# A decoder trunk with a product-key expert layer: one-hot tables compared in batches, the early expert rows summed through diagonal matrices

## The chip, the core and the metric

The kernel runs on one NeuronCore of a Trainium2 chip. The core has five engines that run side by side, each through its own list of instructions in order, and that meet only at semaphores: TensorE (PE: matrix products; PEld is its loading of weights), VectorE (DVE), ScalarE (ACT), GpSimd (POOL) and SyncE (SP, which here issues transfers). Sixteen DMA engines move data between the device memory and the on-chip memory SBUF; PSUM banks take the products of PE. The metric is the device time of one execution in microseconds (us), lower is better, as the median of several runs.

## What is computed

Two layers over 512 tokens of width 1024, in float32. Each layer runs four mixers (state space, linear recurrence, RWKV-7, sparse attention) and then the expert layer (PEER). Only the expert layer is touched:

```python
def peer_ffn(x, wq, keys, u, v):
    ...
    q = (xt @ wq).reshape(t, PEER_HEADS, 2, PEER_KEY_DIM)
    sc = jnp.einsum('thcd,hcnd->thcn', q, keys).astype(jnp.float32)
    s1, i1 = lax.top_k(sc[:, :, 0], PEER_TOPK)
    s2, i2 = lax.top_k(sc[:, :, 1], PEER_TOPK)
    cand = (s1[..., :, None] + s2[..., None, :]).reshape(t, PEER_HEADS, PEER_TOPK * PEER_TOPK)
    cidx = (i1[..., :, None] * PEER_NKEYS + i2[..., None, :]).reshape(t, PEER_HEADS, PEER_TOPK * PEER_TOPK)
    top, pos = lax.top_k(cand, PEER_TOPK)
    eidx = jnp.take_along_axis(cidx, pos, axis=-1)
    gate = jax.nn.softmax(top, axis=-1)
    ...
        act = jax.nn.gelu(jnp.einsum('td,tkd->tk', xb, u[ib]))
        return jnp.einsum('tk,tkd->td', gb * act, v[ib])
```

Each of the 512 tokens picks 128 of 16384 experts (8 heads, 16 each: the best 16 of the 256 sums of 16 and 16 key scores). An expert is a row of `u` and a row of `v`, 1024 floats each; the token's output is the sum over its picks of gate times gelu(x·u) times v.

## The kernel before

The expert layer of one layer is the function `experts`, run once per layer. Its four chunks of 128 tokens are treated in two ways at once.

**Sparse chunks 0 and 1.** There are 256 *steps*, one for each chunk and pick. In a step POOL gathers, for each of the 128 tokens of the chunk, the row of its expert (u and v together, 8 KB) with one indirect DMA of 1 MB (`gather`, L1795) into one of 7 slots; DVE forms the product with x and its sum (`dot`, L1958), ACT takes the gelu of two steps at a time (L1889), and 4 steps later (LAG) DVE multiplies the gate in (L1966) and adds coefficient times v row to the sum `h` (`add_row`, L1970). The gather of step n+3 waits until the sum of step n-4 has freed its slot.

**Dense chunks 2 and 3.** All experts are computed in 128 *tiles* of 128 experts: PE multiplies the tile's u with the 256 tokens (`with_u`, L1848), ACT takes the gelu (L1895), DVE multiplies with the tile's gates (L1978), PE multiplies with the tile's v into banks 4 to 7 (`with_v`, L1859). A u tile and a v tile of 512 KB each are loaded for each. The gates, mostly zeros, are made beforehand in 64 *quads* of 4 tokens: for each token two one-hot tables of 128x128, `hot1` (comparison of an iota with the first key index, times the gate) and `hot2` (comparison with the second key index), and PE multiplies one with the other (`spread_quad`, L1837). ACT copies the result out (L1915), every fourth quad 1 MB goes to device memory (`gates`), and the dense tiles read it back by expert. Of a quad's `hot1`, DVE makes two tables (L1950) and POOL two (L1805), each in one instruction with comparison and gate; `hot2` is made by ACT as relu(1 - (i - n)²), four squares (L1903) and one relu (L1907).

**Order.** All engines walk through the same 212 *beats*, an order written out by numbers: `choose_chunk` (top 16 of the sums and their expert indices, on DVE) of chunk 0 ahead of the beats, of chunk 2 from beat 0, of chunk 3 from beat 14, of chunk 1 from beat 84, in 14 pieces, a piece in each beat; quads in beats 16 to 79; tiles' v products from beat 84; `steps_until(beat)` and `u_until(beat)` say how many steps and u tiles are done by a beat: a step in two of three beats of the quads, 20 u tiles ahead of the dense part, one in every three beats up to beat 60. Within a beat each engine's list has its own order. On POOL: its half of `hot1` of the quad, then the gather. On PE: the quad, then a u tile, then a v tile. On DVE: the piece of the choice, its half of `hot1`, dot, sum, gate of a tile. Within two quads the tables and banks alternate: `hot1` of quad q waits for the product of quad q-2 (`spread`), and the product of q waits for the copy of q-2.

Of the kernel before, what the change touches and what calls it, by code (L numbers as in the profile page):

```python
# [21 lines left out]
P = 128  # L22
# [1473 lines left out]
PICKS = HEADS * TOP  # L1496
ORDER = (0, 2, 3, 1)
# [7 lines left out]
ACTS = 22  # L1505
OWN_ACTS = 14
RUN_AHEAD = 20
# [20 lines left out]
def steps_until(beat):  # L1528

    chosen = CHOOSE_AT[3] + PIECES  # L1530
    if beat <= TILES_AT - 4:
        return max(beat, 0) // 3 + max(beat - chosen, 0) // 3
    first = (TILES_AT - 4) // 3 + (TILES_AT - 4 - chosen) // 3 + 4
    if beat <= TILES_AT:
        return first + beat - TILES_AT
# [120 lines left out]
def choose_chunk(nc, k, p, s, dve, mark, settle, t):  # L1656
# [6 lines left out]
    mark(nc.vector.tensor_tensor(p.sums[:, :, :, :], best[:, :, 0, :].unsqueeze(3).to_broadcast([P, HEADS, TOP, TOP]),  # L1663
                                 best[:, :, 1, :].unsqueeze(2).to_broadcast([P, HEADS, TOP, TOP]), ALU.add))
    settle()
    yield
    rest = p.rest[:, :, :].rearrange("p n w -> p (n w)").rearrange("p (n w) -> p n w", n=2)
    for first in range(0, HEADS, 2):
        heads = range(first, first + 2)
        values = {h: p.sums[:, h, :, :].rearrange("p a b -> p (a b)") for h in heads}  # L1670
        for h in heads:
            mark(nc.vector.max(out=p.top[:, h, 0:8], in_=values[h]))
        settle()
        for h in heads:
            nc.vector.max_index(out=p.where[:, h, 0:8], in_max=p.top[:, h, 0:8], in_values=values[h])
            mark(nc.vector.match_replace(out=rest[:, h % 2, :], in_to_replace=p.top[:, h, 0:8], in_values=values[h], imm_value=-3.0e38))
        settle()
        for h in heads:
            mark(nc.vector.max(out=p.top[:, h, 8:16], in_=rest[:, h % 2, :]))
        settle()  # L1680
        for h in heads:
            mark(nc.vector.max_index(out=p.where[:, h, 8:16], in_max=p.top[:, h, 8:16], in_values=rest[:, h % 2, :]))
        settle()
        yield
# [4 lines left out]
    mark(nc.vector.tensor_scalar(p.rank[:, 0, :], flat, 4, None, ALU.logical_shift_right))  # L1689
# [37 lines left out]
def experts(nc, k, p, A, l):  # L1727
# [3 lines left out]
    with stage(nc, "dve_done", "shifted", "exps", "indexed", "chosen", "turned", "kept", "hot1", "hot1_pool", "squared", "hot2", "spread", "copied",  # L1731
               "stored0", "stored1", "u_done", "gelus_u", "gated", "v_done", "dots", "gelus", "coefs", "summed", "y_added",
# [55 lines left out]
        def _(pool):  # L1788
# [31 lines left out]
        def _(pe):  # L1820
# [8 lines left out]
            def spread_quad(q):  # L1829
                pe.wait_ge(s["hot1"], q + 1)  # L1830
# [31 lines left out]
            for beat in range(BEATS):  # L1862
# [11 lines left out]
        def _(act):  # L1874
# [47 lines left out]
            for beat in range(BEATS):  # L1922
# [10 lines left out]
                if 0 <= beat - QUADS_AT < QUADS:  # L1933
                    second_hots(beat - QUADS_AT)
# [6 lines left out]
        def _(dve):  # L1941
            mark, settle = counted(dve, s["dve_done"])

            def first_hots(q):
# [4 lines left out]
                for n in range(2):  # L1949
# [204 lines left out]
```

## Time and profile before

| | us |
|---|---|
| median of 3 runs | 4028.96 (4024.53 to 4030.17) |
| the profiled execution, its own time | 4015.8 |
| its span, first to last instruction | 4014.1 |
| first layer: choice starts | 778.4 |
| first layer: first and last quad's product start | 867.9, 1102.6 |
| first layer: dense part, first to last v product | 1126.8 to 1986.4 |
| second layer: last quad's product starts | 3099.1 |
| second layer: last v product starts | 3982.0 |

The busy shares of the page (PE 79%, DVE 63%, POOL 27%) are means over stages of different kinds. The expert layers cover some 1210 us of each layer of about 1990, in two clear stages: the quads, in which POOL is the busiest engine, and the dense part, in which the DMA engines are. The page's list of the chain that ended last covers 0% of the span here and says nothing; the stages are read from windows and from the order of instructions in time.

### The profile page before, as it was taken

What the parts mean: (1) busy time and instruction counts of PE and PEld (TensorE: products, weight loads), DVE (VectorE), ACT (ScalarE), POOL (GpSimd) and SP (SyncE); (2) the same over time, 40 slices, a digit from 0 to 9 for tenths busy, and PEclk for the clock granted to TensorE, in tenths of its full rate; (3) what the DMA queues carried; (4) which work ended last, traced back from release to release, by engine and by line L of the source; (5) the groups of instructions that cost most, each with busy time, mean ns of one, the idle gap of its engine ahead of it and who ended that gap; (6) DMA issues with size and microseconds to landing.
All of it is one profiled execution on the core that took longest, in us unless ns stands there. A gap on an engine that the chain in (4) does not pass through costs nothing. (4 is left out here: it accounts for less than half of the span.)

```text
span 4014.1 us, 39261 instructions
## 1 busy us (share of the span) xinstructions
PE 3166.3 (79%) x12836; PEld 2265.1 (56%) x12836; DVE 2544.6 (63%) x5150; ACT 933.6 (23%) x2020; POOL 1102.9 (27%) x1016
## 2 busy tenths in 40 slices
PE   6947677737689999999678477776476899999995
PEld 5725566636556665666266255665365566656662
DVE  3674544896686666666646645348966866666666
ACT  2331133137800000000033311231487000000000
POOL 0012111238922222222200121122498222222221
PEclk9969688868689999999889796888686999999997
DMA  3100112149899999999821001121498999999997
GB/s 103 49 0 1 46 34 82 58 143 317 288 356 411 417 416 417 417 416 406 320 94 37 0 1 46 43 79 58 173 320 284 366 415 417 417 417 417 413 403 303
DMA packets 235342, 943.29 MB, mean 235 GB/s; under 512 B 19584, under 2 KB 85632, under 8 KB 164864
## 3 DMA queue, kind: packets, MB, share of 16 engines
q0 software_dynamic: 73728, 536.90, 33.6%
q1 hardware_dynamic: 95360, 370.31, 24.1%
q10 hardware_dynamic: 66048, 33.56, 2.9%
q8 instruction: 102, 1.67, 0.2%
q14 instruction: 104, 0.85, 0.1%
HBM read 904.52 MB, written 35.65 MB: 234 GB/s over the span
## 5 line engine op out<-in xcount | busy, mean ns | idle before, releaser
L1848 PE MATMUL bank<-peer_x_late,xT 128*128 128x256 f32 x4096 | 987.3, 397 | 146.7 <-ACT peer_acts_u L1895 86.2
L1848 PEld LDWEIGHTS bank<-peer_x_late,xT 128*128 128x128 f32 x4096 | 818.3, 201 | 368.9 <-issue 174.6
L1795 POOL DMA_INDIRECT peer_slots<-in_peer_uv,peer_rows x512 | 542.3, 1059 | 1551.8 <-DVE h L1970 1412.7
L1958 DVE CUSTOM_DVE_ANT_0 peer_slots<-peer_slots,wide 128x1024 f32<-128x1024 f32 x512 | 627.4, 1225 | 512.7 <-DMA peer_slots<-in_peer_uv,peer_rows 511.7
L1970 DVE SCALAR_TENSOR_TENSOR h<-peer_slots,peer_coef,h 128x1024 f32<-128x1024 f32 x512 | 656.9, 1283 | 9.3
L1859 PE MATMUL bank<-ring,peer_acts_u 128*128 128x512 f32 x1344 | 616.9, 605 | 48.6 <-issue 33.3
L1859 PEld LDWEIGHTS bank<-ring,peer_acts_u 128*128 128x128 f32 x1344 | 259.8, 194 | 323.6 <-issue 301.6
L1805 POOL TENSOR_SCALAR peer_hot<-iota,peer_picks 128x128 f32<-128x128 f32 x256 | 329.6, 1294 | 23.7 <-PE bank L1837 20.7
L1837 PE MATMUL bank<-peer_hot 128*128 128x128 f32 x1024 | 195.7, 356 | 176.3 <-ACT peer_hot L1907 65.4
L1889 ACT ACTIVATE peer_coef<-peer_dots 128x2 f32<-128x2 f32 x256 | 51.2, 201 | 1201.1 <-DVE peer_dots L1958 1197.5
L1859 PE MATMUL bank<-ring,wide 128*128 128x512 f32 x704 | 321.1, 601 | 11.3 <-DVE wide L1978 9.9
L1837 PEld LDWEIGHTS bank<-peer_hot 128*128 128x128 f32 x1024 | 175.3, 257 | 195.8 <-issue 138.0
L1859 PEld LDWEIGHTS bank<-ring,wide 128*128 128x128 f32 x704 | 134.6, 192 | 153.5 <-issue 146.3
L1950 DVE TENSOR_SCALAR peer_hot<-iota,peer_picks 128x128 f32<-128x128 f32 x256 | 85.5, 384 | 142.7 <-PE bank L1837 142.0
L190 PE MATMUL bank<-mix_x_hi,w_hi 128*128 128x512 f32 x384 | 154.3, 402 | 12.6 <-DVE w_lo L280 12.6
L1903 ACT ACTIVATE peer_hot<-iota,peer_picks 128x128 f32<-128x128 f32 x512 | 161.9, 390 | 7.4 <-ACT peer_staging L1915 7.3
L1603 POOL TENSOR_TENSOR peer_w_lo<-ring,peer_w_hi 128x1024 fp32r<-128x1024 f32 x32 | 76.4, 2391 | 315.1 <-ACT peer_w_hi L1588 315.1
L191 PE MATMUL bank<-mix_x_lo,w_hi 128*128 128x512 f32 x384 | 153.0, 398 | 0.0
L192 PE MATMUL bank<-mix_x_hi,w_lo 128*128 128x512 f32 x384 | 152.9, 398 | 0.0
L1895 ACT ACTIVATE peer_acts_u<-bank 128x256 f32<-128x256 f32 x168 | 61.8, 378 | 365.9 <-PE bank L1848 363.4
L1915 ACT COPY peer_staging<-bank 128x512 f32<-128x512 f32 x128 | 131.5, 1027 | 57.4 <-PE bank L1837 51.1
L280 DVE TENSOR_TENSOR w_lo<-ring,w_hi 128x1024 fp32r<-128x1024 f32 x48 | 58.6, 1225 | 115.2 <-ACT w_hi L260 115.1
(449 smaller groups left out, 4190.0 us busy)
## 6 DMA issues: line engine op xcount, KB each, us to landing
xT<-in_peer_ut SPq DMA_DIRECT2D x256, 512.0 KB, 18.2
ring<-in_peer_uv SPq DMA_DIRECT2D x256, 512.0 KB, 18.3
gates<-peer_staging ACTq DMA_DIRECT2D x32, 1024.0 KB, 7.1
peer_staging<-gates SPq DMA_DIRECT2D x32, 1024.0 KB, 20.8
ring<-in_w_in SPq DMA_DIRECT2D x48, 512.0 KB, 3.5
ring<-in_peer_wq SPq DMA_DIRECT2D x32, 512.0 KB, 3.5
nsa_w<-in_cmp_w SPq DMA_DIRECT2D x2, 4096.0 KB, 12.1
ring<-in_w_out SPq DMA_DIRECT2D x16, 512.0 KB, 4.2
```

The costliest lines, as they stand in the source:

```text
L190: nc.tensor.matmul(out, left[0], right[0], start=first, stop=False)
L191: nc.tensor.matmul(out, left[0], right[1], start=False, stop=False)
L192: return nc.tensor.matmul(out, left[1], right[0], start=False, stop=last)
L1795: nc.gpsimd.indirect_dma_start(out=p.slots[:, n % ROW_SLOTS, :], out_offset=None, in_=A["peer_uv"], in_offset=bass.IndirectOffsetOnAxis(ap ...
L1805: last = nc.gpsimd.tensor_scalar(p.hot1[:, 4 * (q % 2) + n, :], k.iota128[:, :], p.picks[:, 0, 4 * q + n:4 * q + n + 1], p.picks[:, 2, 4 * ...
L1837: last = nc.tensor.matmul(k.bank[2 + q % 2][:, n * P:(n + 1) * P], p.hot2[:, at, :], p.hot1[:, at, :], start=True, stop=True)
L1848: last = nc.tensor.matmul(k.bank[bank_of[j]][:, 0:DENSE], u_raw[:, j % U_RING, b * P:(b + 1) * P], p.x_late[:, b, :], start=b == 0, stop=b ...
L1859: last = nc.tensor.matmul(k.bank[4 + 2 * t + half][:, :], act_of(j)[:, t * P:(t + 1) * P], k.ring[:, j % V_RING, half * 512:(half + 1) * 5 ...
L1903: last = nc.scalar.activation(hot[:, n, :], k.iota128[:, :], ACT.Square, scale=-1.0, bias=p.picks[:, 1, 4 * q + n:4 * q + n + 1])
L1915: nc.scalar.copy(spread[:, g % 2, :, at:at + 4].rearrange("p j t -> p t j"), k.bank[2 + q % 2][:, :].rearrange("p (t j) -> p t j", t=4)).t ...
L1958: nc.vector.tensor_tensor_reduce(out=u, in0=u, in1=k.wide[:, t, :], scale=1.0, scalar=0.0, op0=ALU.mult, op1=ALU.add, accum_out=p.dots[:, ...
L1970: nc.vector.scalar_tensor_tensor(out=k.h[:, t, :], in0=p.slots[:, m % ROW_SLOTS, DM:2 * DM], scalar=p.coef[:, t, pick:pick + 1], in1=k.h[: ...
```

## The change

There is no change to what goes in and out. `hot1` and `hot2` of a quad are each made by DVE in one comparison of 128x512 (`hots`), without the gate. The gate is then multiplied into the four tables of `hot1` one by one: three by ACT (`gates`, an activation with Copy and a scale), one by POOL (`last_gate`). ACT's squares and relus fall away. PE's product waits for both (`hot1_act`, `hot1_pool`).

For the first 48 steps (EARLY) the sum is no longer DVE's: POOL multiplies the identity with the coefficients of the step (`diagonal`), and PE multiplies this diagonal with the v rows of the slot, adding up in banks 5 and 6 (`add_row` on PE). PE then counts the step as summed. Before the dense tiles DVE adds the two banks to `h` once (`take_early`).

The choice takes the best 16 of 112 sums (the 4 best first keys with all 16 second ones, and the other 12 with the 4 best second ones) rather than of 256, in groups of four heads, with some more small instructions that turn the position into ranks; it has 12 pieces. The numbers of the order: chunk 3 from beat 12, quads in beats 14 to 77, dense tiles from beat 82; a step in three of four beats from beat 24 on (52 steps before the dense part, where there were 47); u tiles one per beat from the start, up to 18, and 20 rather than 22 buffers for activations.

```diff
+PAIRS = 4 * TOP + 12 * 4
...
-ACTS = 22
-OWN_ACTS = 14
-RUN_AHEAD = 20
+ACTS = 20
+OWN_ACTS = 12
+RUN_AHEAD = 18
...
-CHOOSE_AT = {2: 0, 3: 14, 1: 84}
-PIECES = 14
-EXPS_AT = {2: 6, 3: 20, 1: 90}
-TURN_AT = {2: 15, 3: 30}
-KEEP_AT = {2: 16, 3: 31}
-QUADS_AT = 16
-TILES_AT = 84
+CHOOSE_AT = {2: 0, 3: 12, 1: 82}
+PIECES = 12
+EXPS_AT = {2: 4, 3: 16, 1: 86}
+TURN_AT = {2: 12, 3: 24}
+KEEP_AT = {2: 13, 3: 25}
+QUADS_AT = 14
+TILES_AT = QUADS_AT + QUADS + 4
...
+    if beat <= chosen:
+        return beat // 3
+    first = chosen // 3
     if beat <= TILES_AT - 4:
-        return max(beat, 0) // 3 + max(beat - chosen, 0) // 3
-    first = (TILES_AT - 4) // 3 + (TILES_AT - 4 - chosen) // 3 + 4
+        return first + (beat - chosen) * 3 // 4
...
+EARLY = steps_until(TILES_AT) - LAG
+DIAGONALS = 4
...
-        return max(0, min(RUN_AHEAD, (beat + 1) // 3))
+        return max(0, min(RUN_AHEAD, beat))
...
+    sums = p.sums[:, :, :, :].rearrange("p h a b -> p (h a b)")[:, 0:HEADS * PAIRS].rearrange("p (h n) -> p h n", h=HEADS)
+    for at, rows, cols in ((0, slice(0, 4), TOP), (4 * TOP, slice(4, TOP), 4)):
+        n = rows.stop - rows.start
+        mark(nc.vector.tensor_tensor(sums[:, :, at:at + n * cols].rearrange("p h (a b) -> p h a b", b=cols),
+                                     best[:, :, 0, rows].unsqueeze(3).to_broadcast([P, HEADS, n, cols]),
+                                     best[:, :, 1, 0:cols].unsqueeze(2).to_broadcast([P, HEADS, n, cols]), ALU.add))
...
+    for first in range(0, HEADS, 4):
+        heads = range(first, first + 4)
...
+    mark(nc.vector.tensor_scalar(p.rank[:, 0, :], flat, 6, None, ALU.logical_shift_right))
...
-            def first_hots(q):
+            def last_gate(q):
                 if q % (QUADS // 2) == 0:
                     pool.wait_ge(s["kept"], q // (QUADS // 2) + 1)
-                if q >= 2:
-                    pool.wait_ge(s["spread"], q - 1)
-                for n in range(2, 4):
-                    last = nc.gpsimd.tensor_scalar(p.hot1[:, 4 * (q % 2) + n, :], k.iota128[:, :], p.picks[:, 0, 4 * q + n:4 * q + n + 1],
-                                                   p.picks[:, 2, 4 * q + n:4 * q + n + 1], ALU.is_equal, ALU.mult)
-                last.then_inc(s["hot1_pool"], 1)
+                pool.wait_ge(s["hot1"], q + 1)
+                hot = p.hot1[:, 4 * (q % 2) + 3, :]
+                nc.gpsimd.tensor_scalar(hot, hot, p.picks[:, 2, 4 * q + 3:4 * q + 4], None, ALU.mult).then_inc(s["hot1_pool"], 1)
+            def diagonal(m):
+                t, pick = m // PICKS, m % PICKS
+                pool.wait_ge(s["coefs"], m // BATCH + 1)
+                if m >= DIAGONALS:
+                    pool.wait_ge(s["summed"], m - DIAGONALS + 1)
+                nc.gpsimd.tensor_scalar(p.diagonal[:, m % DIAGONALS, :], k.ident[:, :], p.coef[:, t, pick:pick + 1], None,
+                                        ALU.mult).then_inc(s["diagonals"], 1)
...
-                    first_hots(beat - QUADS_AT)
+                    last_gate(beat - QUADS_AT)
                 for n in now(steps_until, beat):
+                    if LAG <= n < LAG + EARLY:
+                        diagonal(n - LAG)
                     if n >= LAG and n - LAG + ROW_SLOTS < STEPS:
                         gather(n - LAG + ROW_SLOTS)
...
-                pe.wait_ge(s["hot1"], q + 1)
+                pe.wait_ge(s["hot1_act"], q + 1)
...
+            def add_row(m):
+                pe.wait_ge(s["diagonals"], m + 1)
+                for half in range(2):
+                    last = nc.tensor.matmul(k.bank[5 + half][:, :], p.diagonal[:, m % DIAGONALS, :],
+                                            p.slots[:, m % ROW_SLOTS, DM + half * 512:DM + (half + 1) * 512],
+                                            start=m == 0, stop=m == EARLY - 1)
+                last.then_inc(s["summed"], 1)
...
+                    pe.wait_ge(s["early_in"], 2)
...
+                for n in now(steps_until, beat):
+                    if LAG <= n < LAG + EARLY:
+                        add_row(n - LAG)
...
-            def second_hots(q):
-
-                hot = p.hot2[:, 4 * (q % 2):4 * (q % 2) + 4, :]
-                if q >= 2:
-                    act.wait_ge(s["spread"], q - 1)
-                for n in range(4):
-                    last = nc.scalar.activation(hot[:, n, :], k.iota128[:, :], ACT.Square, scale=-1.0,
-                                                bias=p.picks[:, 1, 4 * q + n:4 * q + n + 1])
-                last.then_inc(s["squared"], 1)
-                act.wait_ge(s["squared"], q + 1)
-                nc.scalar.activation(hot, hot, ACT.Relu, scale=-1.0, bias=k.ones[:, 0:1]).then_inc(s["hot2"], 1)
+            def gates(q):
+
+                act.wait_ge(s["hot1"], q + 1)
+                for n in range(3):
+                    hot = p.hot1[:, 4 * (q % 2) + n, :]
+                    last = nc.scalar.activation(hot, hot, ACT.Copy, scale=p.picks[:, 2, 4 * q + n:4 * q + n + 1])
+                last.then_inc(s["hot1_act"], 1)
...
-            def first_hots(q):
+            def hots(q):
                 if q % (QUADS // 2) == 0:
                     dve.wait_ge(s["kept"], q // (QUADS // 2) + 1)
                 if q >= 2:
                     dve.wait_ge(s["spread"], q - 1)
-                for n in range(2):
-                    last = nc.vector.tensor_scalar(p.hot1[:, 4 * (q % 2) + n, :], k.iota128[:, :], p.picks[:, 0, 4 * q + n:4 * q + n + 1],
-                                                   p.picks[:, 2, 4 * q + n:4 * q + n + 1], ALU.is_equal, ALU.mult)
-                last.then_inc(s["hot1"], 1)
+                for n, (hot, made) in enumerate(((p.hot1, "hot1"), (p.hot2, "hot2"))):
+                    at = 4 * (q % 2)
+                    nc.vector.tensor_tensor(hot[:, at:at + 4, :], k.iota128[:, :].unsqueeze(1).to_broadcast([P, 4, P]),
+                                            p.picks[:, n, 4 * q:4 * q + 4].unsqueeze(2).to_broadcast([P, 4, P]),
+                                            ALU.is_equal).then_inc(s[made], 1)
...
-                if m:
-                    dve.wait_ge(s["summed"], m)
+                if m < EARLY:
+                    return
...
+            def take_early():
+                dve.wait_ge(s["summed"], EARLY)
+                for half in range(2):
+                    o = slice(half * 512, (half + 1) * 512)
+                    nc.vector.tensor_tensor(k.h[:, 0, o], k.h[:, 0, o], k.bank[5 + half][:, :], ALU.add).then_inc(s["early_in"], 1)
+                dve.wait_ge(s["early_in"], 2)
```

POOL in the middle of the quads, five beats before and four beats after. In `peer_hot` both tables of one-hots are named (here it is `hot1`). Before:

```order
L1805 TENSOR_SCALAR peer_hot<-iota,peer_picks 128x128 x4
L1795 DMA peer_slots<-in_peer_uv,peer_rows 128x2048
L1805 TENSOR_SCALAR peer_hot<-iota,peer_picks 128x128 x2
L1795 DMA peer_slots<-in_peer_uv,peer_rows 128x2048
L1805 TENSOR_SCALAR peer_hot<-iota,peer_picks 128x128 x4
```

After:

```order
L1830 TENSOR_SCALAR peer_hot<-peer_hot,peer_picks 128x128 x2
L1836 TENSOR_SCALAR peer_diagonal<-ident,peer_coef 128x128
L1821 DMA peer_slots<-in_peer_uv,peer_rows 128x2048
L1830 TENSOR_SCALAR peer_hot<-peer_hot,peer_picks 128x128
L1836 TENSOR_SCALAR peer_diagonal<-ident,peer_coef 128x128
L1821 DMA peer_slots<-in_peer_uv,peer_rows 128x2048
L1830 TENSOR_SCALAR peer_hot<-peer_hot,peer_picks 128x128
```

One table a quad stands where two stood, and a diagonal stands directly in front of each gather.

PE at the end of its early u tiles, at the start of the quads (`peer_x_late,xT` is a u tile, eight instructions each; `peer_chosen` the turning of the choice). Before:

```order
L1848 MATMUL bank<-peer_x_late,xT 128x256 x40
L1826 MATMUL bank<-ident,peer_chosen 128x128 x3
L1837 MATMUL bank<-peer_hot 128x128 x4
L1848 MATMUL bank<-peer_x_late,xT 128x256 x8
L1837 MATMUL bank<-peer_hot 128x128 x12
```

After:

```order
L1880 MATMUL bank<-peer_x_late,xT 128x256 x96
L1858 MATMUL bank<-ident,peer_chosen 128x128 x3
L1880 MATMUL bank<-peer_x_late,xT 128x256 x16
L1869 MATMUL bank<-peer_hot 128x128 x4
L1887 MATMUL bank<-peer_slots,peer_diagonal 128x512 x2
L1880 MATMUL bank<-peer_x_late,xT 128x256 x8
L1869 MATMUL bank<-peer_hot 128x128 x4
```

Twelve u tiles stand ahead of the first turning rather than five, 14 ahead of the first quad, and a step's sum follows its beat's quad.

## Rows read from the trace of the kernel before

**Rows 1.** Windows of 50 us, first layer: busy us of each engine, clock, DMA.

```profile
core 0: us, PE busy (x) PEld busy (x) DVE busy (x) ACT busy (x) POOL busy (x), PEclk, DMA share, GB/s
800.00:850.00 50.00, 15.17 (x48) 12.05 (x48) 48.67 (x93) 3.74 (x6) 8.22 (x7) 0.62 0.44 168
...
1050.00:1100.00 50.00, 27.95 (x110) 24.53 (x111) 31.29 (x61) 40.15 (x88) 47.96 (x37) 0.50 0.80 265
...
1300.00:1350.00 50.00, 50.00 (x178) 33.48 (x177) 33.89 (x51) 3.13 (x13) 12.18 (x13) 1.00 1.02 417
```

**Rows 2.** PE through the quads in time: start, us, what, idle before and releaser.

```profile
907.11 2.04 PE L1837 MATMUL bank<-peer_hot 128*128 128x128 f32 x8 [2.64 <-ACT peer_hot L1907]
...
912.94 1.95 PE L1837 MATMUL bank<-peer_hot 128*128 128x128 f32 x16
...
928.26 1.13 PE L1837 MATMUL bank<-peer_hot 128*128 128x128 f32 x8 [2.76 <-ACT peer_hot L1907]
929.23 3.62 PE L1848 MATMUL bank<-peer_x_late,xT 128*128 128x256 f32 x16
```

**Rows 3.** The last quads and the four beats behind them, PE, POOL and DVE in time.

```profile
1095.81 2.75 POOL L1805 TENSOR_SCALAR peer_hot<-iota,peer_picks 128x128 f32<-128x128 f32 x2
...
1098.66 2.05 PE L1837 MATMUL bank<-peer_hot 128*128 128x128 f32 x8 [2.38 <-issue]
...
1102.60 2.04 PE L1837 MATMUL bank<-peer_hot 128*128 128x128 f32 x8 [1.89 <-issue]
...
1106.04 1.28 DVE L1970 SCALAR_TENSOR_TENSOR h<-peer_slots,peer_coef,h 128x1024 f32<-128x1024 f32 x1
...
1107.59 0.94 POOL L1795 DMA_INDIRECT peer_slots<-in_peer_uv,peer_rows  x1 [2.23 <-DVE h L1970]
```

**Rows 4.** POOL in time: the first tables, and the steady order in the quads.

```profile
860.12 3.14 POOL L1805 TENSOR_SCALAR peer_hot<-iota,peer_picks 128x128 f32<-128x128 f32 x4
...
929.66 1.02 POOL L1795 DMA_INDIRECT peer_slots<-in_peer_uv,peer_rows  x1 [0.16 <-issue]
930.73 2.51 POOL L1805 TENSOR_SCALAR peer_hot<-iota,peer_picks 128x128 f32<-128x128 f32 x2
```

**Rows 5.** PE in the dense part: the v products of two tiles.

```profile
1150.07 3.60 PE L1859 MATMUL bank<-ring,peer_acts_u 128*128 128x512 f32 x8
```

**Rows 6.** Groups of instructions of the whole run, with mean ns of one.

```profile
L1805 POOL TENSOR_SCALAR peer_hot<-iota,peer_picks 128x128 f32<-128x128 f32 x256 | 329.6, 1294 | 23.7 <-PE bank L1837 20.7
...
L1903 ACT ACTIVATE peer_hot<-iota,peer_picks 128x128 f32<-128x128 f32 x512 | 161.9, 390 | 7.4 <-ACT peer_staging L1915 7.3
...
L1978 DVE TENSOR_TENSOR peer_acts_u<-peer_acts_u,peer_staging 128x256 f32<-128x256 f32 x168 | 70.1, 419 | 20.4 <-DMA peer_staging<-gates 20.4
...
L1699 DVE TENSOR_TENSOR peer_sums<-peer_rank_f,iota 128x2048 f32<-128x2048 f32 x16 | 36.7, 2291 | 0.1
```

**Rows 7.** DVE: ranking of 128 columns, then the choice of chunk 0, in time.

```profile
774.83 0.87 DVE L1648 MAX8 peer_best<-peer_rest 128x8 f32<-128x128 f32 x4
...
778.36 2.29 DVE L1663 TENSOR_TENSOR peer_sums<-peer_best 128x2048 f32<-128x2048 f32 x1 [1.48 <-PEq L71]
780.69 0.75 DVE L1672 MAX8 peer_top<-peer_sums 128x8 f32<-128x256 f32 x2
...
784.89 0.75 DVE L1672 MAX8 peer_top<-peer_sums 128x8 f32<-128x256 f32 x2
...
812.59 0.29 DVE L1711 TENSOR_SCALAR peer_chosen<-peer_chosen,first_row 128x128 f32<-128x128 f32 x1
...
814.24 2.29 DVE L1663 TENSOR_TENSOR peer_sums<-peer_best 128x2048 f32<-128x2048 f32 x1
```

**Rows 8.** PE before the quads: two u tiles, the turning, the first quad.

```profile
840.59 9.41 PE L1848 MATMUL bank<-peer_x_late,xT 128*128 128x256 f32 x32 [34.83 <-ACT peer_acts_u L1895]
853.95 0.55 PE L1826 MATMUL bank<-ident,peer_chosen 128*128 128x128 f32 x3 [3.95 <-DVE peer_chosen L1722]
867.86 2.08 PE L1837 MATMUL bank<-peer_hot 128*128 128x128 f32 x8 [13.37 <-DVE peer_hot L1950]
```

More of the change, by code:

```diff
@@ L1515 @@
 READ = 8
[L1518 to L1524 removed]
+CHOOSE_AT = {2: 0, 3: 12, 1: 82}
[5 more added lines that the diff above has]
+TILES_AT = QUADS_AT + QUADS + 4
 BEATS = TILES_AT + TILES
 def steps_until(beat):
+    beat = max(beat, 0)
     chosen = CHOOSE_AT[3] + PIECES
+    if beat <= chosen:
+        return beat // 3
+    first = chosen // 3
     if beat <= TILES_AT - 4:
[L1532 to L1533 removed]
+        return first + (beat - chosen) * 3 // 4
+    first += (TILES_AT - 4 - chosen) * 3 // 4
     if beat <= TILES_AT:
[L1535 removed]
+        return first + beat - (TILES_AT - 4)
+    first += 4
     return first + (min(beat, BEATS) - TILES_AT) * (STEPS - first) // TILES
+EARLY = steps_until(TILES_AT) - LAG
+DIAGONALS = 4
 def u_until(beat):
     if beat <= TILES_AT:
[L1542 removed]
+        return max(0, min(RUN_AHEAD, beat))
     return min(TILES, RUN_AHEAD + beat - TILES_AT)
@@ L1662, in choose_chunk @@
     gate = (p.gate[:, t, :] if sparse else p.chosen[:, 2, :]).rearrange("p (h k) -> p h k", k=TOP)
-    mark(nc.vector.tensor_tensor(p.sums[:, :, :, :], best[:, :, 0, :].unsqueeze(3).to_broadcast([P, HEADS, TOP, TOP]),
-                                 best[:, :, 1, :].unsqueeze(2).to_broadcast([P, HEADS, TOP, TOP]), ALU.add))
+    sums = p.sums[:, :, :, :].rearrange("p h a b -> p (h a b)")[:, 0:HEADS * PAIRS].rearrange("p (h n) -> p h n", h=HEADS)
[4 more added lines that the diff above has]
+                                     best[:, :, 1, 0:cols].unsqueeze(2).to_broadcast([P, HEADS, n, cols]), ALU.add))
     settle()
     yield
[L1667 to L1670, printed above, removed]
+    rest = p.rest[:, :, 0:PAIRS]
+    for first in range(0, HEADS, 4):
+        heads = range(first, first + 4)
+        values = {h: sums[:, h, :] for h in heads}
         for h in heads:
@@ L1675, in choose_chunk @@
             nc.vector.max_index(out=p.where[:, h, 0:8], in_max=p.top[:, h, 0:8], in_values=values[h])
-            mark(nc.vector.match_replace(out=rest[:, h % 2, :], in_to_replace=p.top[:, h, 0:8], in_values=values[h], imm_value=-3.0e38))
+            mark(nc.vector.match_replace(out=rest[:, h % 4, :], in_to_replace=p.top[:, h, 0:8], in_values=values[h], imm_value=-3.0e38))
         settle()
         for h in heads:
-            mark(nc.vector.max(out=p.top[:, h, 8:16], in_=rest[:, h % 2, :]))
+            mark(nc.vector.max(out=p.top[:, h, 8:16], in_=rest[:, h % 4, :]))
         settle()
         for h in heads:
-            mark(nc.vector.max_index(out=p.where[:, h, 8:16], in_max=p.top[:, h, 8:16], in_values=rest[:, h % 2, :]))
+            mark(nc.vector.max_index(out=p.where[:, h, 8:16], in_max=p.top[:, h, 8:16], in_values=rest[:, h % 4, :]))
         settle()
@@ L1692, in choose_chunk @@
     settle()
-    mark(nc.vector.tensor_copy(p.rank_f[:, :, :], p.rank[:, :, :]))
+    mark(nc.vector.tensor_scalar(p.rank[:, 0, :], p.rank[:, 0, :], -12.0, 15.0, ALU.mult, ALU.add))
+    settle()
+    mark(nc.vector.tensor_tensor(p.rank[:, 1, :], p.rank[:, 1, :], p.rank[:, 0, :], ALU.bitwise_and))
+    settle()
+    mark(nc.vector.tensor_scalar(p.rank[:, 0, :], flat, 4, None, ALU.logical_shift_right))
+    settle()
+    mark(nc.vector.tensor_copy(p.rank_f[:, :, :], p.rank[:, :, :]))
+    settle()
+    mark(nc.vector.tensor_scalar(p.rank[:, 1, :], flat, 2, None, ALU.logical_shift_right))
+    settle()
+    mark(nc.vector.tensor_scalar(p.wide_rank[:, :], p.rank[:, 1, :], -12.0, None, ALU.add))
+    settle()
+    mark(nc.vector.tensor_tensor(p.rank_f[:, 0, :], p.rank_f[:, 0, :], p.wide_rank[:, :], ALU.max))
     settle()
@@ L1727, in experts @@
 def experts(nc, k, p, A, l):
-    with stage(nc, "dve_done", "shifted", "exps", "indexed", "chosen", "turned", "kept", "hot1", "hot1_pool", "squared", "hot2", "spread", "copied",
-               "stored0", "stored1", "u_done", "gelus_u", "gated", "v_done", "dots", "gelus", "coefs", "summed", "y_added",
+    with stage(nc, "dve_done", "shifted", "exps", "indexed", "chosen", "turned", "kept", "hot1", "hot2", "hot1_act", "hot1_pool", "spread", "copied",
+               "stored0", "stored1", "u_done", "gelus_u", "gated", "v_done", "dots", "gelus", "coefs", "diagonals", "summed", "early_in", "y_added",
                "g_in0", "g_in1", *[f"u_in{n}" for n in range(U_RING)], *[f"v_in{n}" for n in range(V_RING)]) as (block, s):
@@ L1933, in _ @@
                 if 0 <= beat - QUADS_AT < QUADS:
-                    second_hots(beat - QUADS_AT)
+                    gates(beat - QUADS_AT)
                 if 0 <= beat - 1 - QUADS_AT < QUADS:
@@ L1986, in _ @@
                 if 0 <= beat - QUADS_AT < QUADS:
-                    first_hots(beat - QUADS_AT)
+                    hots(beat - QUADS_AT)
+                if beat == TILES_AT:
+                    take_early()
                 for n in now(steps_until, beat):
@@ L2044, in peer @@
         p.hot2 = sb("peer_hot2", [P, HOTS, P])
+        p.diagonal = sb("peer_diagonal", [P, DIAGONALS, P])
         p.staging = sb("peer_staging", [P, 2 * P * GROUP])
```

3 lines of the change are left out of this document (2 added, 1 removed).

## The prediction

> **What bounds the kernel now.** I read the windows first, then the engines in time. From beat 84 on, in the dense part, the DMA engines are busy for all of a window, at 417 GB/s, while DVE is busy for 34 of 50 us; the same holds for nearly all of its 860 us [rows 1]. There, only bytes moved out of the part save time. Ahead of it lie the quads, where no one thing is full all along: in the last ones POOL is busy for 48 of 50 us and the DMA engines for 0.80 [rows 1]. The beat is read from PE: the tenth quad starts at 907.11 [rows 2], the 64th at 1102.60 [rows 3], 54 beats in 195.5 us, **3.62 us a beat**. Ahead of the quads DVE is full (48.7 of 50 us) with choices [rows 1]; PE waits 13.4 us for DVE's first table [rows 8]. So I cost three stretches of a layer, start to tenth quad, 54 beats, dense part, and take both layers as alike (the windows of the second read alike).
>
> **Ahead of the tenth quad.** One choice takes DVE 35.9 us without steps (778.36 to 814.24) [rows 7]. The sums shrink from 2048 columns to 512 and 384: by 1.04 ns a column and 0.42 us for 256 columns [rows 6], about 1.1 us rather than 2.3. The top 16 go in groups of two heads of 256 columns, 4.2 us each (780.69 to 784.89) [rows 7], four of them 16.8 us. For 112 columns the nearest row is the ranking of key scores on 128: four maxima in 0.87 us, where two of 256 columns take 0.75 [rows 7], 0.58 for each; a little under that makes the 16.8 some 9.4. Six small settled instructions come in at 0.3 us each (812.59, 0.29) [rows 7], 1.8 us. A choice becomes 35.9 - 1.2 - 7.4 + 1.8 = 29.1 us. Chunk 0 and chunk 2 stand in series ahead of the quads, so DVE could be through with the second 13 us earlier, at about 841 rather than at the turning of 853.95 [rows 7, 8].
>
> PE can't follow. 12 u tiles now stand ahead of the turning and 14 ahead of the first quad, five before. A tile takes 3.6 us at full clock, 4.7 after a pause (9.41 for two) [rows 2, 8]. ACT frees their banks, and its list holds it at DVE's dots until about 829; from there seven tiles, the first slow, end at about 855, so the turning comes at 855 rather than 853.95 [rows 8] and DVE idles some 5 us. From there DVE has nine pieces of the choice of chunk 3 (18.6 us), ten pairs of comparisons (0.69 us each, so 13), four dots and the waits for PE with its four u tiles among the first quads: the tenth quad starts at about **897** rather than 907.11. That is -10 us, between -20 (PE never late) and 0 (u tiles at half clock).
>
> **54 beats.** POOL's work falls from two tables to one plus 0.75 diagonals, of 0.785 us each undisturbed (3.14 for four) [rows 4], and ACT loses four squares of 0.39 us and a relu. That would make the beat shorter. But a **ring of waits** comes in, read from the lists of the two engines. In a beat with a step POOL does: gate table q, diagonal m, then gather m+7, which waits until row m is summed. PE does: quad q (waits for the gate table), sum of row m. And gate table q+1 stands behind the gather on POOL. Before, the sum was DVE's, next to the dot, and POOL mostly found it done (the wait behind the quads, when it comes, is 2.2 us) [rows 3]. Now nothing of this overlaps with the next beat. At full clock:
> - gate table 0.79 [rows 4] and 0.10 to PE's start (POOL ends at 98.56, PE starts at 98.66) [rows 3];
> - quad, from its start to the next work of PE: 0.97 (928.26 to 929.23) [rows 2]; the diagonal lies beside it;
> - two products of 128x512, four records. Eight take 3.60, seven distances of 0.43 and a last of 0.59 [rows 5]; four take 1.88;
> - 0.27 to the gather (sum ends at 1107.32, gather starts at 1107.59) [rows 3], the gather 1.02 and 0.05 to the next table [rows 4].
>
> Sum 5.08, I say 5.0 to 5.1. A beat without a step adds a second quad, 1.0. Four beats: 3 x 5.05 + 1.0 = 16.2, **4.04 a beat**, against 3.62 now. This is a floor.
>
> Two things raise it. First the clock: in the stretch from 907 to 930, with u tiles among them, a quad takes 2.04 after a pause of 2.64, two take 1.95 behind a u tile, and one takes 1.13 after a pause of 2.76 [rows 2]; in the last quads, without u tiles, the clock is 0.50 throughout [rows 1, 3], with PE busy 28 of 50 us. In the ring PE works 2.85 and idles 2.2, less than both those pauses. At the low level all of the 2.85 doubles (2.04 against 1.0 for a quad) [rows 2] and a step beat would be 7.9; I take one burst in eight at it, 0.35 a step or 0.26 a beat. Second, GpSimd's tables take more than the 0.785 where DVE runs dots and sums beside them (a pair 2.51 and 2.75, a mean of 1.29) [rows 3, 4, 6]. In the ring DVE's comparisons start when a quad ends, and its dot behind them, while POOL mostly waits; I take 0.1 a beat of the possible 0.5. Together 4.04 + 0.26 + 0.1 = **4.4 a beat**, between 4.04 and 5.2. The 54 beats take 237.6 rather than 195.5: **+42**, between +23 and +85.
>
> The DMA work of such a beat is below that: now 0.80 of 3.62 is 2.9 us with two thirds of a gather; a twelfth of a gather more at 417 GB/s (1.05 MB, 2.5 us) makes 3.1 [rows 1].
>
> On this the Trainium skill has a rule (SBUF — State Buffer, Who interferes with whom): a VectorE instruction with two SBUF inputs shuts out a GpSimd instruction that reads SBUF, whichever comes second waiting for the whole of the other. The change makes the comparisons of just that form. The long pairs beside dots and sums agree with it. By the rule alone, with all comparisons in POOL's way, the beat would be 4.5 at full clock; the ring speaks for most of them falling where POOL waits.
>
> **Dense part.** Its steps fall from 209 to 204: 5 x 1.05 MB at 417 GB/s = -12.6 us. Two fewer u tiles are ahead: +2.5. **-10** a layer [rows 1]. The four beats between quads and dense part, the gates' way out and back, and the tail stay as they are. Work of the third choice (chunk 1) hides under the transfers.
>
> **Sum.** -10 + 42 - 10 = +22 a layer, +44 for both. The profiled execution took 4015.8, inside 0.4% of the median of 4028.96; differences are added to the median: **4073 us**. The point from which the sign turns is a beat of 215.7/54 = 3.99 us: just below the floor of the ring.
>
> **Rivals.**
> - *Nothing gained or lost* (0.15): full clock, no disturbance, beat 4.04; 2 x (-10 + 23 - 10) = +6: 4035. For it: two quads in a row at full clock [rows 2]. Against: the low level in the last quads.
> - *Faster* (0.22): the ring is not what sets the beat, since POOL's gather waits in the time in which its next table would have waited anyway, or PE's sum ends earlier than the records say; the beat stays at what other engines need, 3.6, and the front gains 10 to 15: 2 x (-12 - 1 - 10) = -46: 3983. It decides below 3.99 a beat. For it: POOL, the busiest engine, loses 0.2 us a beat and ACT over 1 us. Against: the lists allow no overlap.
> - *Slower through the clock* (0.12): PE stays at the low level in half of the bursts; step beat 6.4, beat 5.2: 2 x (-5 + 85 - 10) = +140: 4169.
> - *The relief isn't one* (0.13): each of seven POOL instructions in four beats pays the 0.5 us that they pay now, on top of the mixed clock: the change frees POOL of a table and gives back its time; beat 4.8 to 4.9: 2 x (-10 + 67 - 10) = +94: 4123. The rule above is its mechanism.
> - *Forecast* (0.38): 4073, its own range 4050 to 4100.
>
> Faster and slower mean here by over 0.2% (8 us), about what a measurement of this kernel can tell from no change. Faster 0.22; the first rival gives 0.10 of its chance to "same" and 0.05 to slower, the forecast's low edge 0.03 to "same": same 0.13, slower 0.65. The range of 8 in 10 leaves out half of the faster rival and most of the clock one: 3990 to 4145.
>
> **What would show it.** In the profile after: GpSimd idle ahead of each gather in the quads for PE's sum (1.8 to 3 us, some 45 times a layer); step beats of 5 us and more with PE idle 2 us ahead of each quad for POOL; 54 beats of 4.4 us; DMA share near 0.75 there; the tenth quad near 897; the turning near 855 with DVE idle before the first comparison; the dense part 10 us shorter at 417 GB/s. Wrong it would be if the beat stays at 3.6, if PE waits for ACT rather than for POOL, or if the dense part grows.

## The result: slower by 2.7%, lost in the quads

The changed kernel takes 4141.26 us (median of four runs, 4127.73 to 4149.91) beside 4029.57 (4024.53 to 4038.63) for the kernel before: a ratio of 1.0272, 95% interval 1.0237 to 1.0306. Forecast were 4073 us and a loss of 44; measured is a loss of 112. The sign and the ring of waits were right. The size was off by a factor of 2.5: the time lies only 4 us inside the upper end of the range (3990 to 4145) and outside the 4050 to 4100 that the forecast gave itself.

The page of the profile after, first the busy shares, then the slices that answer to those of the page before:

```profile
PE 3351.4 (81%) x13220; PEld 2318.9 (56%) x13220; DVE 2461.9 (60%) x5114; ACT 816.8 (20%) x1764; POOL 917.6 (22%) x984
...
PEclk9969688887789999999989696888888999999998
DMA  3100112266679999999921001123666899999997
```

DVE, ACT and POOL all have less to do, and the slices in which the DMA engines are at 6 to 8 tenths are mostly the quads, which had 8 and 9 in the page before, and they grew in number. Cut at the same marks as in the forecast (start of the choice; tenth quad; 64th quad; first v product; end of the last one), in us:

| | layer 1 before | after | layer 2 before | after | difference, forecast |
|---|---|---|---|---|---|
| choice to tenth quad | 128.7 | 118.8 | 128.8 | 119.1 | -10, -10 |
| 54 beats | 195.5 | 273.4 | 195.2 | 262.7 | +78 and +67, +42 |
| 64th quad to first v product | 24.2 | 30.4 | 23.7 | 29.7 | +6, 0 |
| dense part | 859.6 | 847.2 | 859.9 | 847.3 | -12.5, -10 |

The four rows add up to +113 us over both layers, about what the medians differ by. The two profiled executions differ by 123 us. The other 9 lie ahead of the first choice, in stages that the change does not touch: the choice starts at 778.4 before and 787.5 after, and in the seven kernels of the experiments at 778 to 779 three times and at 785.6 to 786.7 four times, whatever was changed in them. Why is open. The stages ahead of the second choice take 789 us in both.

GpSimd in the quads of the kernel after, in time (start, us, what, idle before and its releaser), answering to [rows 4]. L1821 is the gather, L1830 the gate table (the gate multiplied into one table of `hot1`), L1836 the diagonal:

```profile
1006.40 1.00 POOL L1821 DMA_INDIRECT peer_slots<-in_peer_uv,peer_rows  x1 [4.32 <-PE bank L1887]
1007.44 0.63 POOL L1830 TENSOR_SCALAR peer_hot<-peer_hot,peer_picks 128x128 f32<-128x128 f32 x1
1008.03 0.61 POOL L1836 TENSOR_SCALAR peer_diagonal<-ident,peer_coef 128x128 f32<-128x128 f32 x1
1012.96 1.01 POOL L1821 DMA_INDIRECT peer_slots<-in_peer_uv,peer_rows  x1 [4.33 <-PE bank L1887]
```

And TensorE beside it, answering to [rows 2]. L1869 is the quad's product, L1887 the row sum:

```profile
1001.62 2.04 PE L1869 MATMUL bank<-peer_hot 128*128 128x128 f32 x8 [2.33 <-ACT peer_hot L1946]
1003.44 2.68 PE L1887 MATMUL bank<-peer_slots,peer_diagonal 128*128 128x512 f32 x4
1008.17 1.78 PE L1869 MATMUL bank<-peer_hot 128*128 128x128 f32 x8 [2.04 <-issue]
1009.74 2.94 PE L1887 MATMUL bank<-peer_slots,peer_diagonal 128*128 128x512 f32 x4
```

Read as one list, this is the ring of the forecast: gather until 1007.40, gate table until 1008.07, quad from 1008.17, row sum until 1012.68, gather from 1012.96, a step beat of 6.56 us. A step beat is a beat with a step in it. Each engine waits for the other in turn: GpSimd 4.3 us for the sum, TensorE 2.0 us for gather and gate table. (The releaser "issue" ahead of the quad at 1008.17 is GpSimd's gate table, which ends 0.10 earlier.) Over the whole run GpSimd waits so ahead of 96 gathers, 48 a layer, 4.1 us on the mean where 1.8 to 3 was forecast:

```profile
L1821 POOL DMA_INDIRECT peer_slots<-in_peer_uv,peer_rows x512 | 531.8, 1039 | 1779.1 <-DVE h L2012 1273.6 <-PE bank L1887 392.9 <-DVE peer_rows L1739 91.6
L1887 PE MATMUL bank<-peer_slots,peer_diagonal 128*128 128x512 f32 x384 | 252.3, 793 | 18.8 <-POOL peer_diagonal L1836 18.8
```

The beat rose from 3.62 to 5.06 (second layer 4.86), where 4.4 was forecast. The second row shows the missing piece: a record of the row sum takes 793 ns on the mean, while the shortest take 592, as do most of them in the kernel with a granted clock of 1.00 below.

### The profile page after: what moved, and what is told of

The parts are those of the page before. It is cut to its first block and busy times, and to the rows that moved or that the text cites. A ratio compares the mean times of both kernels' runs of the same rounds, so it can differ in the third digit from the quotient of the medians.

```text
span 4136.7 us, 39801 instructions
## 1 busy us (share of the span) xinstructions
PE 3351.4 (81%) x13220; PEld 2318.9 (56%) x13220; DVE 2461.9 (60%) x5114; ACT 816.8 (20%) x1764; POOL 917.6 (22%) x984
## 5 line engine op out<-in xcount | busy, mean ns | idle before, releaser
L1880 PE MATMUL bank<-peer_x_late,xT 128*128 128x256 f32 x4096 | 942.7, 385 | 100.9 <-DMA xT<-in_peer_ut 52.0
L1880 PEld LDWEIGHTS bank<-peer_x_late,xT 128*128 128x128 f32 x4096 | 788.5, 193 | 315.9 <-issue 147.9
L1821 POOL DMA_INDIRECT peer_slots<-in_peer_uv,peer_rows x512 | 531.8, 1039 | 1779.1 <-DVE h L2012 1273.6
L1900 PE MATMUL bank<-ring,peer_acts_u 128*128 128x512 f32 x1280 | 579.4, 597 | 11.1 <-DVE peer_acts_u L2027 9.9
L2012 DVE SCALAR_TENSOR_TENSOR h<-peer_slots,peer_coef,h 128x1024 f32<-128x1024 f32 x416 | 533.6, 1283 | 7.6
L1900 PEld LDWEIGHTS bank<-ring,peer_acts_u 128*128 128x128 f32 x1280 | 243.7, 191 | 264.8 <-issue 251.0
L1991 DVE TENSOR_TENSOR peer_hot<-iota,peer_picks 128x512 f32<-128x512 f32 x256 | 165.5, 689 | 316.0 <-PE bank L1869 309.9
L1900 PE MATMUL bank<-ring,wide 128*128 128x512 f32 x768 | 345.9, 595 | 6.8 <-DMA ring<-in_peer_uv 6.5
L1869 PE MATMUL bank<-peer_hot 128*128 128x128 f32 x1024 | 187.6, 350 | 191.6 <-issue 122.4
L1869 PEld LDWEIGHTS bank<-peer_hot 128*128 128x128 f32 x1024 | 166.6, 250 | 268.5 <-issue 179.0
L1887 PE MATMUL bank<-peer_slots,peer_diagonal 128*128 128x512 f32 x384 | 252.3, 793 | 18.8 <-POOL peer_diagonal L1836 18.8
L1887 PEld LDWEIGHTS bank<-peer_slots,peer_diagonal 128*128 128x128 f32 x384 | 95.2, 274 | 105.9 <-issue 77.8
L1946 ACT ACTIVATE peer_hot<-peer_hot,peer_picks 128x128 f32<-128x128 f32 x384 | 124.5, 389 | 20.9 <-DVE peer_hot L1991 12.5
```

The lines of the kernel that those rows point to most:

```text
L1821: nc.gpsimd.indirect_dma_start(out=p.slots[:, n % ROW_SLOTS, :], out_offset=None, in_=A["peer_uv"], in_offset=bass.IndirectOffsetOnAxis(ap ...
L1869: last = nc.tensor.matmul(k.bank[2 + q % 2][:, n * P:(n + 1) * P], p.hot2[:, at, :], p.hot1[:, at, :], start=True, stop=True)
L1880: last = nc.tensor.matmul(k.bank[bank_of[j]][:, 0:DENSE], u_raw[:, j % U_RING, b * P:(b + 1) * P], p.x_late[:, b, :], start=b == 0, stop=b ...
L1887: last = nc.tensor.matmul(k.bank[5 + half][:, :], p.diagonal[:, m % DIAGONALS, :], p.slots[:, m % ROW_SLOTS, DM + half * 512:DM + (half + ...
L1900: last = nc.tensor.matmul(k.bank[4 + 2 * t + half][:, :], act_of(j)[:, t * P:(t + 1) * P], k.ring[:, j % V_RING, half * 512:(half + 1) * 5 ...
L1991: nc.vector.tensor_tensor(hot[:, at:at + 4, :], k.iota128[:, :].unsqueeze(1).to_broadcast([P, 4, P]), p.picks[:, n, 4 * q:4 * q + 4].unsqu ...
```

## Experiments

Times and ratios are those of each kernel and of the kernel before, run beside it (medians 4021.0 to 4025.61). Theory: the ring of waits (gate table, quad, row sum, gather, next gate table) sets the beat, and TensorE works most of its share of it with the clock at its low level for a part of the burst. Rivals: the comparisons with two SBUF inputs shut GpSimd out; or TensorE's clock is a bound of its own, ring or not; or the clock plays no part.

### Break the ring and keep all the work

```diff
                     if LAG <= n < LAG + EARLY:
                         diagonal(n - LAG)
+                        if n > LAG:
+                            gather(n - LAG - 1 + ROW_SLOTS)
+                        continue
+                    if n == LAG + EARLY:
+                        gather(n - LAG - 1 + ROW_SLOTS)
                     if n >= LAG and n - LAG + ROW_SLOTS < STEPS:
                         gather(n - LAG + ROW_SLOTS)
```

> The changed kernel, but on GpSimd the gather that stood behind a diagonal is put one step later: in the beat of step n it does diagonal m and then the gather that waits for the sum of row m-1, which is long done. All arithmetic is the same. Theory (the ring gate table, quad, sum, gather, gate table sets the beat): the idle time of GpSimd ahead of a gather (4.3 us in each step beat) goes, the 54 beats from the tenth quad to the last take 3.3 to 4.0 us each rather than 5.07, 60 to 95 us less a layer, time about 3950 to 4025. Rival one (TensorE's low clock alone is the bound, 4 quads of 1.84 and 3 sums of 3.75 us in 4 beats): beat 4.65, time about 4095. Rival two (the comparisons with two SBUF inputs shut GpSimd out and set the beat): beat stays at about 5, time 4140.

Measured: 3998.73 us, ratio to the kernel before 0.9918 (0.9898 to 0.9938). The 54 beats take 3.81 us each, in the second layer 3.78. The gather put one step later in GpSimd's list takes 142 us off the changed kernel. The two rivals that were on record fall: all comparisons and all row sums are still there, and their beats of 4.65 and 5 did not come. But the granted clock rose as well (0.79 before the edit, see below), so this run alone doesn't tell ring and clock apart:

```profile
1000.00:1050.00 50.00, 35.72 (x144) 22.24 (x143) 29.75 (x52) 24.14 (x58) 31.93 (x32) 0.90 0.84 278
```

The columns are the busy us of PE, PEld, DVE, ACT and POOL, each with its instructions, then the granted clock, the DMA engines' share and GB/s. The waits of the stretch from 920 to 1090 us (who waited for whom: us, times, longest) name what is late next:

```profile
ACT peer_coef L1938 <- DVE peer_dots L2004: 57.6, 17, 5.0
DVE peer_slots L2004 <- DMA peer_slots<-in_peer_uv,peer_rows: 55.5, 25, 4.6
POOL peer_diagonal L1836 <- DVE peer_coef L2012: 39.5, 16, 4.2
```

GpSimd's wait for TensorE's sum ahead of a gather falls from 96 times 4.1 us to 20 times 1.0 over the run; in its place VectorE waits for rows, since they are asked for one step later, and ScalarE and GpSimd wait for its dots.

### Give TensorE useless work in its pauses

```diff
                 last.then_inc(s["summed"], 1)
+                if m >= 3:
+                    for _ in range(7):
+                        nc.tensor.matmul(k.bank[7][:, 0:P], k.ident[:, :], k.ones[:, :], start=True, stop=True)
```

> The changed kernel with seven products of 128x128 added on TensorE behind each row sum of the early steps, into a bank that nobody reads before it is overwritten: useless work of about 1.5 us at the full clock, in the place where TensorE idles 2.0 us for GpSimd. Theory (the ring, and most of its excess over the forecast is that TensorE works its 2.85 us at the low level for most of each burst: quad and sum take 4.5 us): with more work in its pauses TensorE stays at the full clock, quad and sum fall to 2.9 us, a step beat from 6.56 to 5.1 us and the mean beat from 5.07 to about 4.1, time about 4035 to 4060, faster although work was added. Rival (the level is not what makes quad and sum long, or more work does not raise it): the added work is in the way where it is longer than the pause, beat 5.1 to 6, time 4140 to 4240.

Measured: 4049.57 us, ratio 1.005 (1.003 to 1.0069). Work was added, and the kernel is 92 us faster than the changed one. The window of the changed kernel, then of this one:

```profile
1000.00:1050.00 50.00, 33.05 (x109) 19.83 (x110) 18.69 (x34) 18.21 (x42) 19.61 (x26) 0.79 0.69 216
```

```profile
1000.00:1050.00 50.00, 41.90 (x256) 31.84 (x255) 25.89 (x47) 22.45 (x52) 25.30 (x30) 1.00 0.74 249
```

And TensorE in time, with the added products as the row of 14 records:

```profile
1005.17 1.13 PE L1869 MATMUL bank<-peer_hot 128*128 128x128 f32 x8 [1.48 <-issue]
1006.14 1.88 PE L1887 MATMUL bank<-peer_slots,peer_diagonal 128*128 128x512 f32 x4
1007.86 1.72 PE L1893 MATMUL bank<-ones,ident 128*128 128x128 f32 x14
1010.07 1.13 PE L1869 MATMUL bank<-peer_hot 128*128 128x128 f32 x8 [0.48 <-issue]
```

With 1.72 us of work in a pause of 2.2, the granted clock is 1.00 (2.4 GHz) in each window from 950 us to the end of the quads. Quad and sum take 2.85 us as the forecast's sum had them, and the step beat is 4.90 (1005.17 to 1010.07): the floor of the ring. The 54 beats take 4.22 us each, in the second layer 4.18. So of the changed kernel's 5.06, 0.85 go with the clock and 4.2 stay at full clock; in the second layer, of 4.86, 0.68 go with it. The added work is not in the way: TensorE still idles 0.48 us ahead of the quad at 1010.07. GpSimd still waits for TensorE ahead of 96 gathers, 2.97 us on the mean. As moving the gather took the beat from 4.2 at full clock to 3.8 at 0.90, the ring is a cause of its own beside the clock.

### Take the row sums off TensorE

The early sums go back to VectorE as before: `diagonal`, TensorE's `add_row` and `take_early` fall away, the rest of the change stays.

```diff
-                if m < EARLY:
-                    return
-                dve.wait_ge(s["summed"], m)
+                if m:
+                    dve.wait_ge(s["summed"], m)
```

> The changed kernel with the sums of the early steps back on VectorE, as in the kernel before: no diagonals, no row sums on TensorE, no addition of the two banks. Batched comparisons, gates on ScalarE and GpSimd, the shorter choice and the order by beats stay. Theory (the ring through TensorE is the loss, the rest is a gain): beat 3.3 to 3.7, time about 3960 to 4000. Rival (comparisons with two SBUF inputs, or the gates behind them in the chain VectorE, ScalarE or GpSimd, TensorE, set the beat): beat 4.3 or more, time over 4080.

Measured: 3936.4 us, ratio **0.977** (0.975 to 0.979): faster than the kernel before by 89 us and than the changed one by 205. The beat is 3.21 us. What is left of the change is thus a gain. The choice alone is worth 19 us of it (below); the rest belongs to the comparisons and gates together with the new order of steps and u tiles, and how it splits between these was not tested. The window again:

```profile
1000.00:1050.00 50.00, 30.02 (x122) 25.81 (x121) 48.54 (x72) 28.82 (x67) 34.23 (x27) 0.53 0.95 325
```

VectorE is now full (48.5 of 50 us) and the DMA engines nearly (0.95), while TensorE sits at the low clock (0.53) and costs next to nothing: in the 173 us of the 54 beats VectorE waits 4.7 us for it. The low level that was dear inside the ring is cheap outside it. GpSimd is disturbed beside VectorE's instructions with two SBUF inputs: the gate table at 1001.20 takes 2.03 us rather than 0.63, with VectorE's comparisons beside it until 1001.71 and its dot from 1001.63 to 1002.85. On the mean of the run a gate table takes 1.45 us, 0.77 in the changed kernel:

```profile
999.95 0.63 POOL L1830 TENSOR_SCALAR peer_hot<-peer_hot,peer_picks 128x128 f32<-128x128 f32 x1
1001.20 2.03 POOL L1830 TENSOR_SCALAR peer_hot<-peer_hot,peer_picks 128x128 f32<-128x128 f32 x1 [0.63 <-DVE peer_hot L1985]
```

That agrees with what the Trainium skill says of such pairs (SBUF — State Buffer, Who interferes with whom). It doesn't set this beat, in which VectorE is full.

### Only the choice

The kernel before with the choice among 112 sums and the numbers of the order that go with it.

```diff
-CHOOSE_AT = {2: 0, 3: 14, 1: 84}
-PIECES = 14
+CHOOSE_AT = {2: 0, 3: 12, 1: 82}
+PIECES = 12
...
-QUADS_AT = 16
-TILES_AT = 84
+QUADS_AT = 14
+TILES_AT = 82
...
```

> The kernel before with one part of the change alone: the choice among 112 sums in 12 pieces, and with it chunk 3 from beat 12, quads from beat 14, dense part from beat 82. One-hots, gates, sums, u tiles and the share of steps in the quads stay as before. Theory: each choice takes 29.2 rather than 35.9 us, two of them lie ahead of the quads, so 12 to 16 us a layer come off and the beat stays at 3.6: time about 3998 to 4008. Rival (what is gained ahead of the quads is given back in them, since the quads beside the third choice wait for something else): 4020 to 4030.

Measured: 4006.7 us, ratio 0.9949 (0.9928 to 0.997). The time is as expected. The tenth quad comes 114 us after the start of the choice (128.7 before). But the beat did not stay at 3.6: it is 3.74, so that nearly half of this gain is given back in the 54 beats, which the theory did not have.

### u tiles spread again

On top of the sums on VectorE:

```diff
-        return max(0, min(RUN_AHEAD, beat))
+        return max(0, min(RUN_AHEAD, (beat + 1) // 3))
```

> The changed kernel with the early sums on VectorE (as in e3) and in addition the u tiles spread as in the kernel before: one in three beats rather than one in each beat from the start. Theory (12 u tiles ahead of the turning hold it up: 75 us from the start of the choice to the turning, 61.3 in the run of the choice alone; VectorE then waits a few us, and the rest it fills with the third choice): the turning comes 13 us earlier, the tenth quad 3 to 9 us earlier, the u tiles then lie in the quads, where TensorE has room: 3 to 9 us less a layer than e3, time 3918 to 3932. Rival (the u tiles in the quads are in the way of the quads' products, or the DMA engines, busy for 0.94 there, have no room for their loads): beat 3.4 rather than 3.2, time 3940 to 3960.

Measured: 3954.92 us, ratio 0.9846 (0.9824 to 0.9867), slower than the 3936.4 without this edit, and so the rival. The turning does come 13.7 us earlier (61.3 us after the start of the choice rather than 75.0), but the beat is 3.41 rather than 3.21. The DMA engines are full for a part of the quads:

```profile
950.00:1000.00 50.00, 35.82 (x180) 30.40 (x179) 43.91 (x65) 29.31 (x70) 32.76 (x26) 0.86 1.00 363
```

Twelve u tiles ahead of the turning delay it, and are still the better place for them. Whether their loads or their products are in the way in the quads was not told apart.

### Row sums with the old one-hots

VectorE's and GpSimd's two tables each and ScalarE's squares and relu, with the row sums on TensorE.

```diff
-            def last_gate(q):
...
+            def first_hots(q):
...
+                for n in range(2, 4):
+                    last = nc.gpsimd.tensor_scalar(p.hot1[:, 4 * (q % 2) + n, :], k.iota128[:, :], p.picks[:, 0, 4 * q + n:4 * q + n + 1],
+                                                   p.picks[:, 2, 4 * q + n:4 * q + n + 1], ALU.is_equal, ALU.mult)
```

> The changed kernel with the one-hots made as in the kernel before (VectorE and GpSimd two tables each with the gate in the same instruction, ScalarE squares and relu), but the row sums of the early steps on TensorE through GpSimd's diagonals, and the rest of the order, as in the change. Theory (the ring of waits comes from the row sums alone, and two tables of 0.79 to 1.29 us stand in it where one of 0.63 stood): step beat 7.2 to 7.8 us, beat 5.5 to 6.0, time 4170 to 4250. Rival (the ring needs the comparison on VectorE ahead of GpSimd's gate): beat 3.8 to 4.3, time 4030 to 4070.

Measured: 4244.38 us, ratio 1.0561 (1.0536 to 1.0586); the 54 beats take 5.88 us each. The ring needs nothing of the new one-hots. Two tables stand in it now, and GpSimd shows it:

```profile
999.40 1.60 POOL L1831 TENSOR_SCALAR peer_hot<-iota,peer_picks 128x128 f32<-128x128 f32 x2
1000.99 0.60 POOL L1839 TENSOR_SCALAR peer_diagonal<-ident,peer_coef 128x128 f32<-128x128 f32 x1
1006.85 1.02 POOL L1821 DMA_INDIRECT peer_slots<-in_peer_uv,peer_rows  x1 [5.26 <-PE bank L1890]
```

### Half of the sums on TensorE

Every second early sum is VectorE's, and GpSimd issues two gathers at a time. The edit on GpSimd; the sums of TensorE and VectorE skip every second step accordingly, and each waits for the one before it:

```diff
                     if LAG <= n < LAG + EARLY:
-                        diagonal(n - LAG)
+                        m = n - LAG
+                        if m % 2 == 0:
+                            diagonal(m)
+                        else:
+                            gather(m - 1 + ROW_SLOTS)
+                            gather(m + ROW_SLOTS)
+                        continue
...
```

> The changed kernel with every second early sum on VectorE, every second on TensorE, and GpSimd's gathers two at a time, behind the VectorE sum, so that none waits for a product of TensorE of its own beat. Theory (without the ring the beat goes by what is fullest: in e3 VectorE, 48.5 of 50 us at 3.2 us a beat): VectorE needs 2.8 a beat, the DMA engines 3.1; beat 3.1 to 3.3, time 3915 to 3945. Rival (as in e1, gathers that are issued later make VectorE wait for rows, and this costs more than the sums taken from it): beat 3.4 to 3.8, time 3950 to 4000.

Measured: 3989.94 us, ratio 0.9926 (0.9906 to 0.9946), a miss: the beat is 3.79 and 3.80, not 3.1 to 3.3. VectorE is busy for 35 to 36 of 50 us rather than 48.5, so its time was saved, but in the stretch from 930 to 1060 us TensorE waits for the tables, and VectorE for it:

```profile
PEld bank L1875 <- ACT peer_hot L1954: 53.2, 19, 4.7
PE bank L1875 <- POOL peer_hot L1830: 47.3, 13, 4.5
ACT peer_coef L1941 <- DVE peer_dots L2007: 27.9, 12, 3.1
DVE peer_hot L1999 <- PE bank L1875: 19.5, 8, 2.7
```

GpSimd's gate tables now stand behind two gathers in a row, and a sum of VectorE behind one of TensorE. Time and beat fall into the rival's bounds, but by luck: the rival named late rows, and VectorE waits only 5.2 us for rows in this stretch. Which of the waits above carries the 0.6 us a beat over the kernel with all sums on VectorE was not told apart.

## What the prediction had right, and the step that failed

Of the sum -10 + 42 - 10 a layer, the first and the last term came as forecast. The middle term was mis-sized: +78 and +67 us, not +42, and in it the clock.

- **Three stretches, and bytes in the dense part.** Right: -10 forecast, -12.5 measured, at the same 417 GB/s.
- **Ahead of the tenth quad.** Right: -10 forecast and measured. A choice takes 29.2 us (787.48 to some 816.7), 29.1 forecast; the turning comes 75.0 us after the start of the choice, 76.6 forecast, and VectorE idles 2.7 us for the picks where some 5 were forecast. That the u tiles, and not the choice, are last there is shown by the kernel with the choice alone (61.3).
- **The ring.** Right, and shown from both sides: gone with the gather moved (beat 3.81), there with the old one-hots (5.88), and still there at full clock (4.22). The sum at full clock, 5.05 a step beat, measured 4.90 where the clock was full. The difference is the gate table, 0.63 and not 0.79: the single multiplication is shorter than the comparison with multiplication that I took as its nearest row.
- **The clock in the ring.** This is the step that failed, a term of the right sign and of the wrong size. The forecast took one burst in eight at the low level, 0.26 us a beat or 14 us a layer, since the pauses of 2.2 us are shorter than those of 2.64 and 2.76 in [rows 2]. Measured against the kernel with the filler it is 0.85 and 0.68 a beat, 46 and 37 us a layer, which is nearly all of the excess. Of 40 bursts of quad and row sum in the 54 beats, 35 take more than 3 us in the first layer and 27 in the second (the medians of the 40 are 4.5 and 4.2), where 2.85 is the full clock. Two things were missed. [Rows 2] show a quad at full clock behind a pause of 2.76 and one at the low level behind 2.64, so the length of a pause was no measure at all. And a window's granted clock, 0.79 here, is a mean over time that includes the pauses, while the work is in the bursts: at 4.5 rather than 2.85 us these take 1.6 times as long. One burst in eight had no row behind it. One quad of the four in [rows 2] and both in [rows 3] are at the low level, and over the 54 beats of the kernel before 26 quads in the first layer and 27 in the second are longer than at full clock, most of them twice as long. A term priced from that half would have come near the clock rival.
- **GpSimd beside two SBUF inputs.** 0.1 us a beat forecast; the gate tables take 0.77 on the mean over the run against 0.63 undisturbed, so 0.14. Small in the ring, as forecast, since VectorE works while GpSimd waits for TensorE.
- **The four beats behind the quads.** Forecast as unchanged, measured +6 a layer. They hold row sums too, and the same wait ahead of each gather: 2.90 to 4.63 us from 1181 to 1206. A part of the ring that was left out of the count of its beats.
- **The rivals.** The clock rival was right in kind, and the truth (5.06 and 4.86) lies between the forecast's beat of 4.4 and its 5.2. The rival by which the relief isn't one comes as near in number (4.8 to 4.9, 4123 us), but not in mechanism: it needs 0.5 us more for each table and diagonal of GpSimd, and they take 0.14 more (tables) and next to nothing (diagonals, 0.63 on the mean).

## What to carry to other kernels

When work moves to another engine, follow the semaphore that says it is done: a waiting instruction queued in front of the work that the other engine needs next closes a ring, and its length is the sum of all its parts, however idle each engine looks. The ring here was broken by putting the waiting instruction one step later in its list, at the price of some depth of prefetch: VectorE then waited 55.5 of 170 us for rows. Price TensorE's share of such a ring from bursts as the trace has them, not from the mean clock of a window, and keep the parts of a change apart: here the comparisons, the choice and the new order are together worth -2.3%, and the row sums turned that into +2.7%.

## What the hardware showed unexpectedly

- Seven useless products of 128x128 in each pause (1.72 us) brought the granted clock from 0.79 to 1.00 and the kernel from 4141 to 4050 us.
- A clock of 0.53 in the quads of the fastest kernel cost next to nothing: VectorE, which is full there, waited 4.7 of 173 us for TensorE.
- On GpSimd a table of 128x128 takes 0.60 to 0.63 us with one multiplication by a scalar column, 0.79 with comparison and multiplication [rows 4].
